# Moving a kernel's tiles so that both matmul operands start at the same offset modulo 512 bytes

## The chip, the cores and the metric

The kernel runs on one core of a Trainium2 chip. The metric is the device time of one execution in microseconds (us), as the median of several runs. The kernel's engines are TensorE (PE; its weight loads are listed as PEld), VectorE (DVE), ScalarE (ACT), GpSimd (POOL) and SyncE (SP, which only issues transfers here). They read and write the on-chip memory, of which each of the 128 partitions has its own stretch of bytes; a tile is a range of byte addresses, the same in every partition.

## The reference

One decoder layer for 256 tokens of 2048 features, all in float32:

```python
h = x @ w_in + b_in                       # 2048 -> 5120
a = a_val * sigmoid(a_gate)               # 1024 channels
a = silu(layer_norm(causal_conv31(a)))    # depthwise, 31 taps
s = sc_b * causal_conv3(sc_c * sc_h)      # depthwise, 3 taps
x = layer_norm(ALPHA * x + concat(a, s) @ w_out + b_out)
# PEER: 8 heads, 128 x 128 = 16384 experts, 16 chosen per head and token
q = x @ w_q
s = q . sub_keys; top 16 of each half; top 16 of the 256 sums -> experts, gates g
f = sum over chosen (gelu(x . u[expert]) * g) * v[expert]
x = layer_norm(ALPHA * x + f)
```

## The kernel before

The kernel computes the experts densely: it multiplies the tokens with all of u and weights the result with a matrix of gates that is zero for experts not chosen. All weights pass once through the core as a stream of 656 units of 128 x 1024 float32 (512 KB each): 80 units of w_in, 32 of w_out, 32 of w_q, 256 of u, 256 of v.

Every product is made of three matmuls. A float32 value is split into a rounded upper part (type f32r, fast on TensorE) and a rest: w = w_hi + w_lo, x = xt_hi + xt_lo. Then hi x hi, hi x lo and lo x hi are added up in the accumulation memory (psum). So each unit of the stream passes four engines: SyncE issues its load into a slot of `raw` (4 slots; from the fifth unit of v on also 3 slots of `raw_late`), ScalarE writes the upper part into one of four tiles `w_hi` (L627), VectorE writes the rest into one of four tiles `w_lo` (L843; GpSimd at L571 for the 32 units of w_q and the first 36 of u), and TensorE uses them. ScalarE may only write a w_hi when TensorE has released it (`used`), SyncE may only fill a raw slot when the rest was taken from it.

TensorE's work by stage, in program order:

- w_in, w_q and u (L1411 to L1413): a matmul loads 128 x 128 of a weight part into the array (the stationary operand, 512 bytes per partition) and streams 256 columns of xt_hi or xt_lo (the moving operand, 1024 bytes per partition). A unit has 24 such matmuls. During w_in, VectorE also computes the taps of the convolutions (L878 to L882, L973 to L997); the output projection waits for its last `mix_lo`.
- w_out (L1460 to L1462): here the loaded operand is mix_hi or mix_lo (128 tokens), and 512 columns of w_hi or w_lo are streamed (2048 bytes). 12 matmuls a unit. Then two layer-normalisation halves and transposes of the result (L1486).
- w_q: between the units the scores (L1500) load q_t and stream keys, 128 columns, two calls at a time, each as two matmuls in the profile.
- u: in the tile number 14 TensorE transposes the selections (L1542), after which every third tile has a batch of eight matmuls in 16-bit types that makes the gates (L1553).
- v, the downward stage (L1587 to L1589): coefficients c_hi, c_lo (128 tokens) are loaded, 512 columns of w are streamed. For half of the columns, only the first 128 tokens are computed this way; for the other 128 tokens GpSimd gathers the 128 chosen coefficients (L588) and rows of v (L582) by indirect transfers, and VectorE adds them up, one pick of 128 x 1024 every other unit or so (L1312). The coefficients come through a copy of `hid` in main memory, dumped by ScalarE's queue. The last four units of the stream do not go to w_hi and w_lo but to tiles of their own, `tail_hi` and `tail_lo` (`parts_of`), on the same lines.

The order within each engine is written out by hand, with semaphores between the engines. Tiles get their addresses in the order of their declaration; an ExitStack that is closed gives its space free for what is declared next, so that tiles of different stages share bytes.

Adding up the declared sizes gives these starts, in bytes modulo 512, of what TensorE reads:

| tiles | before | after |
|---|---|---|
| w_hi0 to 3, w_lo0 to 3 | 0 | 0 |
| xt_hi, xt_lo, mix_hi, mix_lo | 288 | 0 |
| c0 to c4 (hi and lo) | 288 | 0 |
| tail_hi0 to 3, tail_lo0 to 3 | 288 | 0 |
| q_t0, q_t1, oh1, oh2g | 288 | 0 |
| acc | 288 | 0 |
| keys, ident | 96 | 320 |

All steps that the matmuls of the table's first four rows take inside these tiles are multiples of 512 bytes.

Of the kernel before, what the change touches and what calls it, by code (L numbers as in the profile page):

```python
# [5 lines left out]
P = 128  # L6
T = 256
TB = T // P
D = 2048
KT = D // P  # L10
HALF = KT // 2
# [6 lines left out]
N_KEYS = 128  # L18
DCH = 512
NCH = D // DCH  # L20
GROUP = 4
GROUPS = N_KEYS // GROUP
BATCH = 8
INNER = 2
OUTER = BATCH // INNER
# [5 lines left out]
JCOLS = JOINED * DCH  # L31
NB = T // BATCH
PICKS = HEADS * TOPK
ROWS = 4
# [7 lines left out]
PARTS = 2  # L42
# [6 lines left out]
RAW = 4  # L49
SPLIT = 4  # L50
# [68 lines left out]
RAW_LATE = 3  # L119
# [47 lines left out]
def build(nc, x_t, x_nat, w_in, w_out, w_q, u_w, v_w, params, sub_keys, b_out, ln1_g, ln1_b, ln2_g, ln2_b, out):  # L167
    f32 = mybir.dt.float32
    f32r = mybir.dt.float32r
    bf16 = mybir.dt.bfloat16  # L170
    f16 = mybir.dt.float16
# [7 lines left out]
    with ctx:  # L179
        def sb(name, shape, dt, where=ctx):  # L180
            return where.enter_context(nc.sbuf_tensor(name, shape, dt))
# [1 line left out]
        def sem(name):  # L183
            return ctx.enter_context(nc.semaphore(name))

        raw = sb("raw", [P, RAW, HALF * P], f32)
        w_hi = [sb(f"w_hi{i}", [P, HALF * P], f32r) for i in range(SPLIT)]
        w_lo = [sb(f"w_lo{i}", [P, HALF * P], f32r) for i in range(SPLIT)]
        stats = sb("stats", [P, TB, NCH, 6], f32)
        mv = sb("mv", [P, TB, 2], f32)  # L190
        rstd = sb("rstd", [P, TB, 1], f32)
        neg_mean = sb("neg_mean", [P, TB, 1], f32)

        def coefs(name, where):
            return [sb(f"{name}_{part}", [P, GROUP, T], f32r, where) for part in ("hi", "lo")]


        down0 = ExitStack()
        c_sets = [coefs("c0", down0)]
        sp_coef = sb("sp_coef", [P, PICKS], f32, down0)  # L200
        row_late = sb("row_late", [P, JCOLS], f32, down0)
        down0.close()
        iota_t = sb("iota_t", [P, N_KEYS, INNER], f16)
        tab1 = sb("tab1", [P, T], f16)
        tab2 = sb("tab2", [P, T], f16)
        gate_p = sb("gate_p", [P, T], bf16)
        gate_t = sb("gate_t", [P, PARTS, T], f16)
        oh1 = sb("oh1", [P, OUTER, N_KEYS, INNER], bf16)
        gtmp = sb("gtmp", [P, N_KEYS, BATCH], f32)
        oh2g = sb("oh2g", [P, OUTER, PARTS, N_KEYS, INNER], f16)  # L210


        down1 = ExitStack()
        c_sets += [coefs("c1", down1)]
        raw_late = sb("raw_late", [P, RAW_LATE, HALF * P], f32, down1)
        rows = [sb(f"rows{i}", [P, JCOLS], f32, down1) for i in range(ROWS - 1)] + [row_late]
        down1.close()
        xt_hi = sb("xt_hi", [P, KT, T], f32r)
        xt_lo = sb("xt_lo", [P, KT, T], f32r)

        early = ExitStack()
# [48 lines left out]
        down2 = ExitStack()  # L272
        res = sb("res", [P, TB, D], f32, down2)
        ln2g = sb("ln2g", [P, D], f32, down2)
        ln2b = sb("ln2b", [P, D], f32, down2)
        c_sets += [coefs(f"c{i}", down2) for i in (2, 3, 4)]
        tail_hi = [sb(f"tail_hi{i}", [P, HALF * P], f32r, down2) for i in range(SPLIT)]
        tail_lo = [sb(f"tail_lo{i}", [P, HALF * P], f32r, down2) for i in range(SPLIT)]
        down2.close()


        def raw_of(u):
# [5 lines left out]
                return tail_hi[u % SPLIT], tail_lo[u % SPLIT]  # L288
            return w_hi[u % SPLIT], w_lo[u % SPLIT]

        hid = sb("hid", [P, N_KEYS, T], f32)

# [1393 lines left out]
```

## Time and profile before

| | |
|---|---|
| median of 3 runs | 1748.53 us (1746.63 to 1752.34) |
| span of the profiled execution | 1745.8 us (the page gives no device time of it beside the span) |
| TensorE matmul busy | 1713.3 us, 98% |
| TensorE weight load busy | 1578.1 us, 90% |
| VectorE busy | 1407.6 us, 81% |
| ScalarE busy | 854.0 us, 49% |
| GpSimd busy | 540.4 us, 31% |
| moved by transfers | 504.52 MB, mean 289 GB/s |

Busy time of TensorE is to be read with care: matmuls are pipelined, each is shown longer than the distance to the next, so that the engine counts as busy at any rate of issue. What tells the rate is the distance between two starts. A line of the profile names what is written, an arrow, and what is read; an x and a number count the instructions of a group. PEclk is the granted clock, 1.00 being 2.4 GHz.

### The profile page before, as it was taken

To read this page: it belongs to the slowest core of one execution; us is meant where nothing else is said; L and a number is where in the kernel's file an instruction comes from. 1 tells how busy PE (TensorE), PEld (TensorE's weight loads), DVE (VectorE), ACT (ScalarE), POOL (GpSimd) and SP (SyncE) were. 2 spreads that over 40 slices of the span, in tenths; PEclk is the share of its full clock that TensorE was granted. 3 is DMA by queue.
4 is the path that set the end of the run, shared out by engine and by line. 5 is a ranking of instruction groups with operands and counts; after the bars stand their busy time and mean duration, and the time that the engine had idled before them with its cause. 6 is when DMAs were issued, how large, how long until landed. Compare 5 with 4: busy or idle time off the path is not lost.

```text
span 1745.8 us, 31461 instructions
## 1 busy us (share of the span) xinstructions
PE 1713.3 (98%) x11910; PEld 1578.1 (90%) x11910; DVE 1407.6 (81%) x1998; ACT 854.0 (49%) x1084; POOL 540.4 (31%) x342
## 2 busy tenths in 40 slices
PE   8999999899999999999999999999999999999997
PEld 8999987799999999999999999998788777878776
DVE  7999997678967677777777777556899898999997
ACT  5544436344544444444444444445555555555544
POOL 0000000288881000000000000004787777777731
PEclk9999999999999999999999999999999999999999
DMA  7787787777777777777677777899899999999994
GB/s 267 267 276 267 234 260 249 273 237 235 250 249 252 238 236 244 247 235 239 237 241 239 236 244 243 282 355 332 314 400 400 399 401 389 400 399 395 369 398 133
DMA packets 173728, 504.52 MB, mean 289 GB/s; under 512 B 19408, under 2 KB 35920, under 8 KB 172624
## 3 DMA queue, kind: packets, MB, share of 16 engines
q1 hardware_dynamic: 134000, 427.08, 70.0%
q0 software_dynamic: 22528, 67.19, 10.0%
q10 hardware_dynamic: 17120, 9.35, 1.8%
q8 instruction: 29, 0.48, 0.1%
q14 instruction: 51, 0.42, 0.1%
HBM read 490.98 MB, written 79.69 MB: 327 GB/s over the span
## 4 chain that ended last, share of the span: by engine, by line
PE 78%; DMA 6%; DVE 6%; issue 5%; POOL 3%; ACT 1%; DVEq 1%; SPq 0%; POOLq 0%; ACTq 0%
PE psum L1411 18%; PE psum L1413 18%; PE psum L1412 18%; PE psum L1587 6%; PE psum L1589 6%; PE psum L1588 6%; POOL sp_coef L588 2%; DVE w_lo L843 2%; DMA raw<-in_v_w_dram 2%; PE psum L1553 2%; DMA raw_late<-in_v_w_dram 1%; PE psum L1460 1%; PE psum L1462 1%; PE psum L1461 1%; DVE psum L1312 1%
## 5 line engine op out<-in xcount | busy, mean ns | idle before, releaser
L627 ACT ACTIVATE w_hi<-raw 128x1024 fp32r<-128x1024 f32 x547 | 578.9, 1060 | 682.1 <-PE psum L1413 487.1
L1411 PE MATMUL psum<-xt_hi,w_hi 128*128 128x256 f32 x2944 | 827.2, 281 | 5.3 <-DVE xt_lo L857 3.1
L1412 PE MATMUL psum<-xt_lo,w_hi 128*128 128x256 f32 x2944 | 822.6, 279 | 0.0
L1413 PE MATMUL psum<-xt_hi,w_lo 128*128 128x256 f32 x2944 | 822.4, 279 | 0.0
L843 DVE TENSOR_TENSOR w_lo<-raw,w_hi 128x1024 fp32r<-128x1024 f32 x479 | 581.8, 1222 | 221.5 <-ACT w_hi L627 219.7
L1411 PEld LDWEIGHTS psum<-xt_hi,w_hi 128*128 128x128 f32 x2944 | 554.3, 188 | 6.6 <-issue 6.0
L1412 PEld LDWEIGHTS psum<-xt_lo,w_hi 128*128 128x128 f32 x2944 | 554.3, 188 | 0.0
L1413 PEld LDWEIGHTS psum<-xt_hi,w_lo 128*128 128x128 f32 x2944 | 554.1, 188 | 0.0
L582 POOL DMA_INDIRECT rows<-v_rows,sp_idx x96 | 130.9, 1364 | 709.7 <-issue 674.9
L1587 PE MATMUL psum<-w_hi,c_hi 128*128 128x512 f32 x752 | 299.7, 399 | 8.9 <-DVE w_lo L843 8.7
L1589 PE MATMUL psum<-w_hi,c_lo 128*128 128x512 f32 x752 | 298.2, 396 | 0.0
L1588 PE MATMUL psum<-w_lo,c_hi 128*128 128x512 f32 x752 | 297.9, 396 | 0.0
L571 POOL TENSOR_TENSOR w_lo<-raw,w_hi 128x1024 fp32r<-128x1024 f32 x68 | 164.7, 2427 | 364.3 <-ACT w_hi L627 364.2
L588 POOL DMA_INDIRECT sp_coef<-hid_spill,sp_idx x128 | 193.0, 1508 | 55.2 <-issue 45.9
L1587 PEld LDWEIGHTS psum<-w_hi,c_hi 128*128 128x128 f32 x752 | 141.7, 188 | 49.5 <-DVE w_lo L843 15.4
L1589 PEld LDWEIGHTS psum<-w_hi,c_lo 128*128 128x128 f32 x752 | 141.6, 188 | 34.3
L1588 PEld LDWEIGHTS psum<-w_lo,c_hi 128*128 128x128 f32 x752 | 141.7, 188 | 33.3
L627 ACT ACTIVATE w_hi<-raw_late 128x1024 fp32r<-128x1024 f32 x105 | 111.3, 1060 | 103.2 <-PE psum L1589 75.0
L843 DVE TENSOR_TENSOR w_lo<-raw_late,w_hi 128x1024 fp32r<-128x1024 f32 x105 | 126.6, 1221 | 8.4 <-ACT w_hi L627 8.4
L1312 DVE SCALAR_TENSOR_TENSOR psum<-rows,sp_coef,psum 128x1024 f32<-128x1024 f32 x95 | 121.8, 1282 | 3.2 <-DMA rows<-v_rows,sp_idx 2.3
L882 DVE SCALAR_TENSOR_TENSOR cacc<-apad,prm,cacc x232 | 101.3, 480 | 0.0
L1293 DVE TENSOR_TENSOR c_lo<-hid,c_hi 128x1024 fp32r<-128x1024 f32 x32 | 39.2, 1224 | 22.9 <-ACT c_hi L776 22.8
(164 smaller groups left out, 1131.8 us busy)
## 6 DMA issues: line engine op xcount, KB each, us to landing
raw<-in_u_w_dram SPq DMA_DIRECT2D x256, 512.0 KB, 4.2
raw<-in_v_w_dram SPq DMA_DIRECT2D x148, 512.0 KB, 8.7
v_rows<-in_v_w_dram SPq DMA_DIRECT2D x128, 512.0 KB, 5.2
raw_late<-in_v_w_dram SPq DMA_DIRECT2D x108, 512.0 KB, 8.9
raw<-in_w_in_dram SPq DMA_DIRECT2D x80, 512.0 KB, 4.3
raw<-in_w_out_dram SPq DMA_DIRECT2D x32, 512.0 KB, 4.5
raw<-in_w_q_dram SPq DMA_DIRECT2D x32, 512.0 KB, 4.5
hid_spill<-hid ACTq DMA_DIRECT2D x7, 1024.0 KB, 15.4
```

The source lines that it names most:

```text
L571: nc.gpsimd.tensor_tensor(w_lo[s][:, :], raw[:, s, :], w_hi[s][:, :].bitcast(f32), ALU.subtract).then_inc(lo_done[s], SPLIT)
L582: nc.gpsimd.indirect_dma_start(rows[k % ROWS][:, :], None, v_rows, bass.IndirectOffsetOnAxis(sp_idx[:, 1, k:k + 1], 0)).then_inc(rows_in[k ...
L588: nc.gpsimd.indirect_dma_start(sp_coef[:, k:k + 1], None, hid_dram, bass.IndirectOffsetOnAxis(sp_idx[:, 0, k:k + 1], 0)).then_inc(act_in[k ...
L627: nc.scalar.activation(parts_of(slot_u)[0][:, :], raw_of(slot_u), ACT.Copy).then_inc(hi_done, 1)
L843: tt(lo_w[:, :], raw_of(slot_u), hi_w[:, :].bitcast(f32), ALU.subtract).then_inc(lo_done[slot_u % SPLIT], SPLIT)
L1312: i = stt(picked[:, :], rows[k % ROWS][:, :], sp_coef[:, k:k + 1], picked[:, :], ALU.mult, ALU.add)
L1411: mm(dst, hi_w[:, sl], xt_hi[:, kk, :], start=st, stop=False)
L1412: mm(dst, hi_w[:, sl], xt_lo[:, kk, :], start=False, stop=False)
L1413: i = mm(dst, lo_w[:, sl], xt_hi[:, kk, :], start=False, stop=en)
L1587: mm(v_bank(j, b), c1, w1, start=st, stop=False)
L1588: mm(v_bank(j, b), c1, w2, start=False, stop=False)
L1589: i = mm(v_bank(j, b), c2, w1, start=False, stop=en)
```

## The change

The declarations are put in another order, and one tile is added. First come the tiles of the early stages, the routing, the accumulators and the late tiles, which all lie over the space of `hid`, then `hid` itself; behind it raw, w_hi, w_lo and the small tiles, then an unread tile `place_pad` of 56 floats (224 bytes) in each partition, then the tiles of the first coefficient sets and the gates, and xt. The list of coefficient sets has the same order as before. No instruction, wait, transfer or loop differs.

```diff
-        raw = sb("raw", [P, RAW, HALF * P], f32)
-        w_hi = [sb(f"w_hi{i}", [P, HALF * P], f32r) for i in range(SPLIT)]
-        w_lo = [sb(f"w_lo{i}", [P, HALF * P], f32r) for i in range(SPLIT)]
...
-        down0 = ExitStack()
-        c_sets = [coefs("c0", down0)]
...
-        xt_hi = sb("xt_hi", [P, KT, T], f32r)
-        xt_lo = sb("xt_lo", [P, KT, T], f32r)
         early = ExitStack()
...
-        c_sets += [coefs(f"c{i}", down2) for i in (2, 3, 4)]
+        c_late = [coefs(f"c{i}", down2) for i in (2, 3, 4)]
...
         down2.close()
+        hid = sb("hid", [P, N_KEYS, T], f32)
+
+        raw = sb("raw", [P, RAW, HALF * P], f32)
+        w_hi = [sb(f"w_hi{i}", [P, HALF * P], f32r) for i in range(SPLIT)]
+        w_lo = [sb(f"w_lo{i}", [P, HALF * P], f32r) for i in range(SPLIT)]
+        stats = sb("stats", [P, TB, NCH, 6], f32)
+        mv = sb("mv", [P, TB, 2], f32)
+        rstd = sb("rstd", [P, TB, 1], f32)
+        neg_mean = sb("neg_mean", [P, TB, 1], f32)
+        sb("place_pad", [P, 56], f32)
+
+        down0 = ExitStack()
+        c_sets = [coefs("c0", down0)]
...
+        down1 = ExitStack()
+        c_sets += [coefs("c1", down1)] + c_late
...
+        xt_hi = sb("xt_hi", [P, KT, T], f32r)
+        xt_lo = sb("xt_lo", [P, KT, T], f32r)
...
-        hid = sb("hid", [P, N_KEYS, T], f32)
```

## Rows read from the trace of the kernel before

**Rows 1.** The page's head: the profiled span.
```profile
span 1745.8 us, 31461 instructions
```

**Rows 2.** Windows by stage: length, busy time of each engine, PEclk, transfers' share, GB/s.
```profile
core 0: us, PE busy (x) PEld busy (x) DVE busy (x) ACT busy (x) POOL busy (x), PEclk, DMA share, GB/s
...
100.00:246.00 146.00, 145.13 (x1203) 142.88 (x1201) 140.24 (x251) 61.29 (x69) 0.00 (x0) 1.00 0.78 262
...
272.00:323.00 51.00, 51.00 (x219) 41.08 (x220) 34.25 (x35) 26.88 (x30) 0.00 (x0) 1.00 0.85 297
336.00:1168.00 832.00, 831.13 (x7115) 826.08 (x7116) 603.05 (x1050) 383.98 (x604) 155.29 (x64) 1.00 0.75 249
...
1248.00:1625.00 377.00, 371.42 (x1576) 295.98 (x1576) 352.60 (x315) 206.25 (x199) 289.18 (x204) 1.00 1.03 398
...
1650.00:1695.00 45.00, 44.17 (x189) 35.03 (x188) 44.02 (x41) 24.20 (x23) 17.75 (x12) 1.00 1.03 409
1695.00:1735.00 40.00, 39.80 (x172) 31.98 (x171) 30.61 (x37) 19.88 (x22) 5.11 (x4) 1.00 0.48 167
```

**Rows 3.** Waits from 12 to 246 us (first row) and 336 to 1168 (others): total, times, longest.
```profile
DVE apad L947 <- ACT sig L653: 3.6, 4, 1.5
...
ACT w_hi L627 <- PE psum L1413: 401.4, 254, 4.1
...
DVE tab L1219 <- PE psum L1542: 12.9, 1, 12.9
```

**Rows 4.** Timeline of TensorE at the end of the upward stage, first and last of 28.
```profile
1165.75 0.28 PE L1412 MATMUL psum<-xt_lo,w_hi 128*128 128x256 f32 x1
...
1168.90 0.28 PE L1412 MATMUL psum<-xt_lo,w_hi 128*128 128x256 f32 x1
```

**Rows 5.** Waits from 1248 to 1695 us.
```profile
ACT w_hi L627 <- DMA raw<-in_v_w_dram: 33.7, 32, 2.4
...
ACT w_hi L627 <- DMA raw_late<-in_v_w_dram: 24.2, 22, 1.8
```

**Rows 6.** Timeline of TensorE: 21 tail starts, then 24 ordinary, then 19 tail.
```profile
1719.65 0.39 PE L1587 MATMUL psum<-tail_hi,c_hi 128*128 128x512 f32 x1
...
1724.19 0.39 PE L1589 MATMUL psum<-tail_hi,c_lo 128*128 128x512 f32 x1
...
1724.41 0.40 PE L1587 MATMUL psum<-w_hi,c_hi 128*128 128x512 f32 x1
...
1729.78 0.40 PE L1589 MATMUL psum<-w_hi,c_lo 128*128 128x512 f32 x1
...
1731.17 0.39 PE L1589 MATMUL psum<-tail_hi,c_lo 128*128 128x512 f32 x1
...
1735.25 0.39 PE L1589 MATMUL psum<-tail_hi,c_lo 128*128 128x512 f32 x1
```

**Rows 7.** Line 1413: the one ahead of a score batch, and all from 340 to 1168 us.
```profile
L1413 PE MATMUL psum<-xt_hi,w_lo x1: 274/274/274, 360.6 to 360.6; 128*128 128x256 f32 x1
...
L1413 PE MATMUL psum<-xt_hi,w_lo x2255: 274/278/415, 340.0 to 1168.0; 128*128 128x256 f32 x188
```

**Rows 8.** The chain that ended last: start, length, what.
```profile
341.82 1.31 PE psum L1486 x12
...
1186.97 13.88 DMA hid_spill<-hid
...
1238.02 6.26 DMA rows<-v_rows,sp_idx
```

**Rows 9.** Transfers of the weights of v: issuer, count, KB, us to landing.
```profile
raw<-in_v_w_dram SPq DMA_DIRECT2D x148, 512.0 KB, 8.7
...
raw_late<-in_v_w_dram SPq DMA_DIRECT2D x108, 512.0 KB, 8.9
```

More of the change, by code:

```diff
@@ L184, in sem @@
             return ctx.enter_context(nc.semaphore(name))
-        raw = sb("raw", [P, RAW, HALF * P], f32)
-        w_hi = [sb(f"w_hi{i}", [P, HALF * P], f32r) for i in range(SPLIT)]
-        w_lo = [sb(f"w_lo{i}", [P, HALF * P], f32r) for i in range(SPLIT)]
[L189 to L192, printed above, removed]
         def coefs(name, where):
             return [sb(f"{name}_{part}", [P, GROUP, T], f32r, where) for part in ("hi", "lo")]
-        down0 = ExitStack()
-        c_sets = [coefs("c0", down0)]
[L200 to L217, printed above, removed]
-        xt_hi = sb("xt_hi", [P, KT, T], f32r)
-        xt_lo = sb("xt_lo", [P, KT, T], f32r)
         early = ExitStack()
@@ L279, in build @@
         down2.close()
+        hid = sb("hid", [P, N_KEYS, T], f32)
[9 more added lines that the diff above has]
+        c_sets = [coefs("c0", down0)]
+        sp_coef = sb("sp_coef", [P, PICKS], f32, down0)
+        row_late = sb("row_late", [P, JCOLS], f32, down0)
+        down0.close()
+        iota_t = sb("iota_t", [P, N_KEYS, INNER], f16)
+        tab1 = sb("tab1", [P, T], f16)
+        tab2 = sb("tab2", [P, T], f16)
+        gate_p = sb("gate_p", [P, T], bf16)
+        gate_t = sb("gate_t", [P, PARTS, T], f16)
+        oh1 = sb("oh1", [P, OUTER, N_KEYS, INNER], bf16)
+        gtmp = sb("gtmp", [P, N_KEYS, BATCH], f32)
+        oh2g = sb("oh2g", [P, OUTER, PARTS, N_KEYS, INNER], f16)
+        down1 = ExitStack()
+        c_sets += [coefs("c1", down1)] + c_late
+        raw_late = sb("raw_late", [P, RAW_LATE, HALF * P], f32, down1)
+        rows = [sb(f"rows{i}", [P, JCOLS], f32, down1) for i in range(ROWS - 1)] + [row_late]
+        down1.close()
+        xt_hi = sb("xt_hi", [P, KT, T], f32r)
+        xt_lo = sb("xt_lo", [P, KT, T], f32r)
         def raw_of(u):
```

## The prediction

> **What bounds the kernel now.** I read the page first, then the windows by stage, the timeline of TensorE, the waits of each stage, and last the chain and the transfers. The page gives a span of 1745.8 us [rows 1]; it shows no other time for that execution, and the three timed runs have their median at 1748.53, so 2.7 us lie around the span or between executions. I work out a saving in microseconds and take it from the median.
>
> The reader is to see in the windows that TensorE never rests for long: from 336 to 1168 us it is busy 831.13 of 832 us at the full granted clock, while VectorE has 603 and ScalarE 384 [rows 2]. In that stage ScalarE waits for TensorE 401.4 us [rows 3]: TensorE sets the time, and every nanosecond between two of its matmuls counts. Busy time hides what matters, though, because matmuls overlap. So I take the step from one start to the next. Twenty-seven steps from 1165.75 to 1168.90 make 3.15 us, 0.1167 us each, for 256 columns, which at 2.4 GHz take 0.1067 [rows 4]. Each matmul costs 10 ns more than its columns.
>
> Three places look different. From 100 to 246 us VectorE is busy 140.24 of 146 us beside TensorE [rows 2]. From 1248 to 1625 us the transfers stand at 398 GB/s with a share of 1.03, after 249 GB/s in the stage before [rows 2], and from 1650 to 1695 at 409. And ScalarE waits there for weights that are still on their way, 33.7 and 24.2 us [rows 5].
>
> **Part one, the addresses.** Nothing is added or removed that runs: same instructions, transfers, waits and queues. The extra tile is never touched. Only addresses move. Adding up the declared sizes (small tiles rounded up to 32 bytes, which the 224 of the diff bears out: 288 + 224 = 512), before the change the split weights start at 0 modulo 512 and everything they meet (xt, mix, c0 to c4) at 288; each step along them is a multiple of 512. Afterwards all are at 0.
>
> **Part two, its price.** The trace holds a pair of cases that differ in just this. The last four units of the stream go to tail_hi and tail_lo, which stand at 288 as c does: equal offsets already. Ordinary units on w_hi and w_lo, with offsets 0 and 288, run right before, same line of code, same c tiles. The ordinary ones take 23 steps from 1724.41 to 1729.78, 0.2335 each; the tail ones 18 steps from 1731.17 to 1735.25, 0.2267 each [rows 6]. That is 6.8 ns less on 512 columns. An earlier pass over the tail tiles, 20 steps from 1719.65 to 1724.19, makes 0.2270 each while VectorE is still splitting weights and normalising, so the quiet of the end isn't the cause.
>
> For 256 columns there is one hint. While a matmul streams, the weights of the next one are loaded. L1413 streams xt_hi (288), and normally w_hi (0) is loaded behind it. Ahead of a score batch it is q_t (288) instead: that matmul took 274 ns, the shortest there is, against a median of 278 [rows 7]. So the price is 4 ns there. Two readings of the tail rows are open: a price per streamed column gives 6.8 / 2 = 3.4 ns, a price per load gives 6.8. The 274 decides for the column reading; I take 3.4.
>
> The Trainium skill speaks against any gain: "TensorE: Matmul & The Clock Gate", Part 2, step 1, says that TensorE has two independent read ports, one for the streamed operand and one for the load, so that loading takes no bandwidth from the running matmul. By that the change saves 0. The 6.8 ns of the tail rows disagree, so it becomes a rival and not the forecast.
>
> **Part three, stage by stage.**
> - *0 to 246 us*, 80 units of 24 matmuls: 1920 x 3.4 = 6.5 us on TensorE. But VectorE's own work does not shrink. It waited for TensorE only through the sigmoids, 3.6 us in all [rows 3]; when these waits are gone it is the bound, and its last mix_lo gates the output projection. A matmul stream that is ahead by 18 to 29 units at these waits has gained 1.5 to 2.4 us there. I count 2 us (bounds 0 and 6.5).
> - *246 to 336 us*: until 272 a chain of VectorE and ScalarE runs beside TensorE; then 219 matmuls follow with TensorE busy 51.00 of 51 us [rows 2]: 219 x 6.8 = 1.5 us, plus some of the first hundred. I count 2 (bounds 1.5 and 384 x 6.8 = 2.6). The normalisation behind it stays.
> - *336 to 1184 us*, queries and upward projection, 288 units: 6912 matmuls x 3.4 = 23.5 us. What hid nothing before hides nothing now: VectorE at 603 of 832 would be at 603 of 809. The one fixed meeting, the selections that TensorE transposes in the fifteenth tile, had VectorE waiting 12.9 us for it [rows 3]; TensorE comes there about 5 us sooner, which uses up less than half. Transfers at a share of 0.75 have room. Bounds 0 and, with 6.8 ns, 47 us.
> - *1184 to 1248 us*, first 64 us of the downward projection: TensorE could gain 1.8 us, but the first picks wait for the dump of hid (landing 1200.85) and for the gathered rows (1238.02 to 1244.28) [rows 8], a chain that hangs on the end of the upward stage and not on TensorE's pace. I count 0.
> - *1248 to 1695 us*: 2.9% less time for the same bytes would want about 398 x 1.03 = 410 GB/s, and the rate stands flat at 398. Faster matmuls wait longer for weights. I count 0 of the stage's roughly 13 us. Would the moved tiles make transfers quicker? Those into raw (offset 0) took 8.7 us to land and those into raw_late (288) 8.9 [rows 9]; both stand in one queue, so I count 0 and allow 3.
> - *1695 to 1735 us*: transfers are down to 167 GB/s and TensorE is free: some 100 ordinary matmuls x 6.8 = 0.7 us. I count 1.
>
> Sum: 2 + 2 + 23.5 + 0 + 0 + 1 = 28.5 us. 1748.5 - 28.5 = 1720 us; the span goes to 1717.
>
> **Rivals.**
> - *The downward stage gains as well.* For: TensorE is busy 371.42 of 377 us there, so it looks like the bound too. Against: the flat rate of transfers. If all its 2256 ordinary matmuls save 6.8 ns that is 15.3 us, and with the whole 6.5 and 2.6 of the first stages (8832 x 3.4 + 384 x 6.8 + 15.3 = 48 us) the time is 1701. Chance of a good part of this (1700 to 1712): 14%.
> - *Less than 3.4 ns, or VectorE becomes the bound sooner.* Half of the price in the long stage gives about 1735. Chance 10% (1728 to 1743).
> - *The price per load, or more.* With 0 and 0 the surplus could vanish down to what a load alone takes. Twelve transposes of 128 columns took 1.31 us, 109 ns each [rows 8]; 116.7 - 109 = 7.7 ns over 6912 matmuls is 53 us, with the other stages about 60: 1688. In the Trainium skill, "TensorE: Matmul & The Clock Gate", the table of the issue gap gives 262 cycles for 256 columns, which would be the same 109; no row here shows a 256-column step so short. Against: the tail pairs, at equal offsets, still pay 13 ns on 512 columns. Chance 5%.
> - *The offset is not what matters.* The tail tiles differ in more than the offset: they lie elsewhere, among other tiles. If that made the 6.8 ns, nothing changes: 1748. Chance 8%. It is also the case in which the Trainium skill (the same page and step) is right about the ports.
> - *Slower.* Equal offsets put both reads on the same boundary at the same time, and 0 may be worse than 288, which is all that the trace shows. The place would be every matmul; were the price as large the other way, 8832 x 3.4 + 2688 x 6.8 = 48 us more, 1797. It decides when the long stage's step is above 0.117. Chance 5%.
>
> **How the numbers follow.** The forecast of 1720 (1712 to 1728) has 58%. The range 1700 to 1735 leaves out the no-effect case, the slower one, the load-bound one and a few of the 10%: about 2 in 10. A change within 0.3% (5 us) is about what a measurement here can't tell from none. Faster by more: 58 + 14 + 10 + 5 = 87%; same 8%; slower 5%.
>
> **What would show it.** The step in the upward stage goes from 0.1167 to 0.1133 (353 starts in 40 us rather than 343 by these steps); the transposes and score batches stay. Where the downward stage is undisturbed the step goes from 0.2335 to 0.2267, but its stalls on w_lo grow and its length hardly falls; the rate of transfers stays near 400. Before 246 us VectorE is busy without a gap and TensorE waits for mix_lo longer than now. I am wrong if the long stage's step does not move, if it falls below 0.112, or if the downward stage becomes 10 us shorter.

## The result, and the profile after

The changed kernel is slower: 1774.11 us (median of 4 runs, 1772.78 to 1778.28) against 1749.43 us for the kernel before beside it (4 runs), a ratio of 1.0139, 95% interval 1.0122 to 1.0156. The forecast was 1720, with a range of 1700 to 1735. The change is under 2%, but the interval lies wholly above 1, so it is a real loss of some 25 us.

The head of the page after, and two of its costliest groups (behind the bar: busy us, mean ns of one, idle us before them and what ended it):

```profile
span 1772.3 us, 31461 instructions
...
L1411 PE MATMUL psum<-xt_hi,w_hi 128*128 128x256 f32 x2944 | 838.0, 285 | 4.7 <-DVE xt_lo L857 2.7
...
L1587 PE MATMUL psum<-w_hi,c_hi 128*128 128x512 f32 x752 | 297.3, 395 | 18.7 <-DVE w_lo L843 16.8
```

The number of instructions is that of [rows 1], and the span is 26.5 us longer. The windows of the kernel after, same stretches and columns as [rows 2]:

```profile
core 0: us, PE busy (x) PEld busy (x) DVE busy (x) ACT busy (x) POOL busy (x), PEclk, DMA share, GB/s
...
100.00:246.00 146.00, 146.00 (x1199) 145.16 (x1198) 136.83 (x243) 59.63 (x67) 0.00 (x0) 1.00 0.78 255
...
272.00:323.00 51.00, 49.91 (x221) 40.99 (x220) 36.00 (x37) 28.48 (x33) 0.00 (x0) 1.00 0.78 268
336.00:1168.00 832.00, 828.86 (x6911) 823.20 (x6912) 593.65 (x1042) 374.25 (x593) 158.08 (x66) 1.00 0.74 239
...
1248.00:1625.00 377.00, 361.11 (x1554) 292.27 (x1553) 346.57 (x309) 203.54 (x196) 284.25 (x203) 0.99 1.01 384
...
1650.00:1695.00 45.00, 44.05 (x194) 35.96 (x193) 42.93 (x39) 24.04 (x24) 33.82 (x21) 1.00 1.02 390
```

From 336 to 1168 us TensorE is busy almost as before (828.86 us where it was 831.13), at the same clock, but 6911 matmuls start where 7115 did. The timeline of the kernel after, the end of the upward stage, then two starts in the downward stage, shows the steps:

```profile
1165.05 0.28 PE L1411 MATMUL psum<-xt_hi,w_hi 128*128 128x256 f32 x1
...
1168.29 0.28 PE L1411 MATMUL psum<-xt_hi,w_hi 128*128 128x256 f32 x1
...
1490.00 0.39 PE L1589 MATMUL psum<-w_hi,c_lo 128*128 128x512 f32 x1
...
1494.76 0.39 PE L1589 MATMUL psum<-w_hi,c_lo 128*128 128x512 f32 x1
```

The first pair has 27 steps in 3.24 us, 0.1200 each: 3.3 ns more than in [rows 4], where 3.4 less was forecast. The second has 21 steps in 4.76 us, 0.2267 each, just the step of the tail tiles in [rows 6]. So equal offsets cost time at 256 columns and save it at 512.

The first start of each stage in the two traces (before 9.44, 235.17, 336.87, 1183.83 and last 1735.25 us; after 9.03, 241.02, 340.92, 1209.69 and 1761.73) divides the difference of the spans (us):

| stage | before | after | difference |
|---|---|---|---|
| first matmul to output projection, 256 columns | 225.7 | 232.0 | +6.3 |
| output projection to queries, 512 columns | 101.7 | 99.9 | -1.8 |
| queries and upward projection, 256 columns | 847.0 | 868.8 | +21.8 |
| downward projection to its last matmul, 512 columns | 551.4 | 552.0 | +0.6 |

They add up to 26.9 us; the first matmul of the kernel after starts 0.4 us sooner. The third row is close to 6912 x 3.33 ns = 23.0 us; the first steps behind each batch and transpose grow by less. In the downward stage the quicker step came to nothing. The waits of the kernel after from 1248 to 1695 us show where it went (total, times, longest); the first and the last had been 12.8 and 7.4 us before:

```profile
PEld psum L1587 <- DVE w_lo L843: 23.7, 25, 4.4
...
ACT w_hi L627 <- DMA raw<-in_v_w_dram: 34.5, 33, 2.4
...
PE psum L1587 <- DVE w_lo L843: 15.0, 13, 4.0
```

TensorE waits longer for split weights. That their raw form is still on its way shows when the stretch is shifted by the 26 us by which the stage starts later: from 1274 to 1721 us ScalarE waits 41.4 and 24.7 us for it, where it was 33.7 and 24.2 [rows 5]. Shifted so, the transfers stand at 395 GB/s, and the kernel before has 396 from 1248 to 1695; the 384 and 390 above are of windows that lie earlier in the stage. VectorE's waits for gathered rows grow from 2.3 to 7.5 us in the stage.

Over the whole stage, what the steps longer than 300 ns take beyond the normal step adds up to 28.6 us, where it was 14.3 before.

A small part of this is the clock. Behind pauses of 4.4 and 3.5 us the granted clock of the kernel after falls to 0.50, the 1.2 GHz level, for 6.8 and 3.4 us, as in this window from it:

```profile
core 0: us, PE busy (x) PEld busy (x) DVE busy (x) ACT busy (x) POOL busy (x), PEclk, DMA share, GB/s
1272.00:1275.00 3.00, 3.00 (x8) 2.31 (x7) 3.00 (x4) 0.69 (x1) 2.39 (x3) 0.50 0.84 260
```

There 512 columns step by 427 ns, which costs 3.9 us of the 28.6. The kernel before has one such stretch, of 3.4 us behind a pause of 2.5 us, which costs 1.5 of its 14.3.

### The profile page after: what moved, and what is told of

Read it like the earlier page. It is cut to its first block, busy times and chain, and to the rows that moved or that the text cites. A ratio compares the mean times of both kernels' runs of the same rounds, so it can differ in the third digit from the quotient of the medians.

```text
span 1772.3 us, 31461 instructions
## 1 busy us (share of the span) xinstructions
PE 1730.0 (98%) x11910; PEld 1606.5 (91%) x11910; DVE 1408.1 (79%) x1998; ACT 854.2 (48%) x1084; POOL 543.3 (31%) x342
## 4 chain that ended last, share of the span: by engine, by line
PE 77%; DMA 8%; DVE 6%; issue 5%; POOL 3%; ACT 1%; DVEq 0%; SPq 0%; POOLq 0%; ACTq 0%
PE psum L1411 20%; PE psum L1412 20%; PE psum L1413 20%; PE psum L1587 4%; PE psum L1589 4%; PE psum L1588 4%; DVE w_lo L843 3%; DMA raw<-in_v_w_dram 2%; POOL sp_coef L588 2%; DMA raw_late<-in_v_w_dram 2%; PE psum L1553 2%; DVE psum L1312 1%; DMA row_late<-v_rows,sp_idx 1%; PE psum L1460 1%; PE psum L1461 1%
## 5 line engine op out<-in xcount | busy, mean ns | idle before, releaser
L1411 PE MATMUL psum<-xt_hi,w_hi 128*128 128x256 f32 x2944 | 838.0, 285 | 4.7 <-DVE xt_lo L857 2.7
L1412 PE MATMUL psum<-xt_lo,w_hi 128*128 128x256 f32 x2944 | 833.4, 283 | 0.0
L1413 PE MATMUL psum<-xt_hi,w_lo 128*128 128x256 f32 x2944 | 833.2, 283 | 0.0
L1411 PEld LDWEIGHTS psum<-xt_hi,w_hi 128*128 128x128 f32 x2944 | 565.3, 192 | 6.0 <-issue 5.4
L1412 PEld LDWEIGHTS psum<-xt_lo,w_hi 128*128 128x128 f32 x2944 | 565.4, 192 | 0.0
L1413 PEld LDWEIGHTS psum<-xt_hi,w_lo 128*128 128x128 f32 x2944 | 565.3, 192 | 0.0
L582 POOL DMA_INDIRECT rows<-v_rows,sp_idx x96 | 152.7, 1590 | 725.8 <-issue 692.5
L1589 PE MATMUL psum<-w_hi,c_lo 128*128 128x512 f32 x752 | 294.3, 391 | 0.0
L588 POOL DMA_INDIRECT sp_coef<-hid_spill,sp_idx x128 | 175.0, 1367 | 56.4 <-issue 47.3
L1588 PEld LDWEIGHTS psum<-w_lo,c_hi 128*128 128x128 f32 x752 | 142.1, 189 | 28.6
```

The lines of the kernel that those rows point to most:

```text
L582: nc.gpsimd.indirect_dma_start(rows[k % ROWS][:, :], None, v_rows, bass.IndirectOffsetOnAxis(sp_idx[:, 1, k:k + 1], 0)).then_inc(rows_in[k ...
L588: nc.gpsimd.indirect_dma_start(sp_coef[:, k:k + 1], None, hid_dram, bass.IndirectOffsetOnAxis(sp_idx[:, 0, k:k + 1], 0)).then_inc(act_in[k ...
L1411: mm(dst, hi_w[:, sl], xt_hi[:, kk, :], start=st, stop=False)
L1412: mm(dst, hi_w[:, sl], xt_lo[:, kk, :], start=False, stop=False)
L1413: i = mm(dst, lo_w[:, sl], xt_hi[:, kk, :], start=False, stop=en)
L1588: mm(v_bank(j, b), c1, w2, start=False, stop=False)
```

## The experiments

Theory 1 says that the step depends on the distance between the two places that TensorE reads at once, the stream's and that of the weights being loaded, and that 0 is bad for 256 columns and good for 512. Its rival, theory 2, puts the time down to the order of the tiles or to what else lies near them.

### The two reads by themselves

A kernel of its own, with no reference work: one tile of weights at offset 0 modulo 512, sixteen tiles to stream, mv_a to mv_p, at 0, 32, ... 480, nothing beside TensorE. Each is streamed with a weight load per matmul, first 64 times 256 columns, then 48 times 512.

```diff
+for mv in mvs:
+    case(mv, 256)      # st[:, k*128:(k+1)*128] loaded, mv[:, k*256:(k+1)*256] streamed
+for mv in mvs:
+    case(mv, 512)
```

> This kernel leaves the layer out and only measures: one loaded tile st at offset 0 modulo 512, sixteen streamed tiles mv_a to mv_p at offsets 0, 32, 64 ... 480, 64 matmuls of 256 columns on each and then 48 of 512 columns on each, with a load of 128 columns before every one, as in the layer; the other engines are idle. Theory 1 (the step depends on the difference of the two offsets, and differently for 256 and for 512 columns): at 256 columns mv_a (0) steps by 120 ns and mv_j (288) by 116.7 on average; at 512 columns mv_a steps by 227, and the offset that stands for 224 (mv_h) by 233.5. Theory 2 (position in the partition or the traffic of other engines makes the difference): all sixteen step alike in each width, within 1 ns. If theory 1 holds, the sweep says which difference is the cheapest for 256 columns; there may be one near 113.

The timeline of this kernel, a group for each tile (start, busy, what):

```profile
71.51 7.42 PE L66 MATMUL psum<-mv_g,st 128*128 128x256 f32 x64
78.77 7.73 PE L66 MATMUL psum<-mv_h,st 128*128 128x256 f32 x64
86.34 7.84 PE L66 MATMUL psum<-mv_i,st 128*128 128x256 f32 x64
94.01 7.71 PE L66 MATMUL psum<-mv_j,st 128*128 128x256 f32 x64
101.56 7.70 PE L66 MATMUL psum<-mv_k,st 128*128 128x256 f32 x64
...
131.88 7.42 PE L66 MATMUL psum<-mv_o,st 128*128 128x256 f32 x64
139.14 7.73 PE L66 MATMUL psum<-mv_p,st 128*128 128x256 f32 x64
...
224.68 11.35 PE L66 MATMUL psum<-mv_h,st 128*128 128x512 f32 x48
235.87 11.05 PE L66 MATMUL psum<-mv_i,st 128*128 128x512 f32 x48
246.75 11.37 PE L66 MATMUL psum<-mv_j,st 128*128 128x512 f32 x48
```

From one group's start to the next: mv_g, 192 bytes off, (78.77 - 71.51) / 64 = 113.4 ns; mv_i, 256 off, 7.67 / 64 = 119.8; mv_j, 288 off, 118.0. With 512 columns mv_i makes 10.88 / 48 = 226.7 and mv_h 233.1. Tiles that are 256 bytes apart behave alike (mv_o as mv_g), so the period is 256 bytes and not 512. Settled steps, the first few matmuls of a tile left out (of mv_a those at the lower clock too), by the distance modulo 256:

| bytes | 0 | 32 | 64 | 96 | 128 | 160 | 192 | 224 |
|---|---|---|---|---|---|---|---|---|
| 256 columns, ns | 120.0 | 117.8 | 117.8 | 120.0 | 118.7 | 117.4 | 113.3 | 118.2 |
| 512 columns, ns | 226.7 | 233.3 | 228.9 | 233.3 | 233.4 | 234.2 | 233.4 | 233.4 |

The layer's 120.0 and 226.7 are both here at distance 0, with nothing else running. That is theory 1, and it leaves VectorE, ScalarE and the transfers out of the cause. One number is a nanosecond off: mv_j has the distance of the kernel before and steps 117.8, while the layer stepped 116.7; the last sweep below finds 116.7 at this distance too.

### The order without the pad

The changed kernel without its pad: everything behind it lies 224 bytes lower, so xt, c0 and c1 are 288 from the weights again, in the new order. The mix tiles, first in the partition, stay at 0.

```diff
-        sb("place_pad", [P, 56], f32)
```

> The changed kernel without its unread tile: the new order of the tiles stays, the difference of the offsets is 288 again for xt, c0 and c1, while mix and c2 to c4 are at 0 as w is. Theory 1 (the difference of offsets): the upward stage steps by 116.7 ns as before and the time comes back to 1749 within 4 us. Theory 2 (the new place in the partition costs the time): the step stays at 120 and the time stays near 1774.

1748.92 us against 1750.94, ratio 0.9989 (0.9975 to 1.0003). The long stage steps 116.67 ns as before; the output projection steps 226.7 and takes 100.0 us, as after, since mix still stands at 0. The order by itself shows no effect.

### Only xt away from the weights

```diff
-        (stats, mv, rstd, neg_mean and place_pad behind the weights)
+        sb("x_pad", [P, 72], f32)
         xt_hi = sb("xt_hi", [P, KT, T], f32r)
         xt_lo = sb("xt_lo", [P, KT, T], f32r)
+        (stats, mv, rstd, neg_mean)
```

Weights, mix and coefficients are all at 0, xt alone at 288.

> The changed kernel with xt_hi and xt_lo alone put back to 288 by 288 unread bytes in front of them (the small tiles stand behind xt, which makes the first unread tile unnecessary); mix and all c stay at 0. Theory 1: the step of 256 columns is 116.7, that of 512 columns 227; the time is that of the kernel before less what the quicker 512-column matmuls give, 2 us in the output projection and 0 to 5 in the downward stage that its transfers bound: 1742 to 1748. If the downward stage is bound by TensorE and not by transfers: 1732. Theory 2 (place): 120 and near 1774.

1748.78 against 1750.94, ratio 0.9985 (0.9974 to 0.9997). Stage by stage it is the kernel before in the two stages on xt (225.6 and 848.7 us, where it was 225.7 and 847.0) and the kernel after elsewhere: 227.1 ns a step with 512 columns and 28.6 us of pauses in the downward stage, which is no shorter (551.9). The time lies just above the 1742 to 1748 expected. The slowdown is xt's offset alone, and the quicker steps at 512 columns are worth 2 us.

### xt at 192, the best distance of the sweep

As above with `x_pad` of 48 floats instead of 72.

> As x_at_288, with 192 unread bytes in front of xt_hi instead of 288: xt lies 192 above w modulo 256, where the sweep had its cheapest 256-column step, and mix and all c stay at the offset of w. Theory 1 (the difference modulo 256 bytes sets the step): 256 columns step by 113.3 ns, so the 288 units from the queries to the end of the upward stage take 848 - 6912 x 0.0034 = 825 us; 512 columns step by 227; the downward stage stays near 551 us, since transfers bind it; the first stage gains 1 to 3 us, since VectorE binds it. Time 1721, between 1717 and 1727. Theory 2 (in the whole layer other engines' traffic disturbs the step, so that the sweep does not carry over): 116 and more, 1745 or above.

1755.41 us against 1749.86, ratio 1.0020 (1.0004 to 1.0036), where 1721 was expected: the 113.3 ns of the sweep did not last. The 12 runs lie between 1746.28 and 1760.22; the one traced took 1759.92. The timeline of this kernel, before the first score batch and then in the upward stage:

```profile
345.04 0.28 PE L1412 MATMUL psum<-xt_lo,w_hi 128*128 128x256 f32 x1
...
347.99 0.28 PE L1411 MATMUL psum<-xt_hi,w_hi 128*128 128x256 f32 x1
...
599.94 0.28 PE L1411 MATMUL psum<-xt_hi,w_hi 128*128 128x256 f32 x1
...
602.77 0.28 PE L1411 MATMUL psum<-xt_hi,w_hi 128*128 128x256 f32 x1
```

The first pair makes 26 steps of 113.5 ns, as the sweep had it. Behind the score batch the stream falls to 24 steps in 2.83 us, 117.9, and stays there for the rest of the stage: same tiles, same addresses, another step. A score batch isn't needed for it. In the first stage, which has none, the same kernel steps 117.8 from 14 to 237 us; as many matmuls start in 40 us there as in the upward stage:

```profile
100.00:140.00 40.00, 40.00 (x342) 40.00 (x341) 39.58 (x65) 16.49 (x19) 0.00 (x0) 1.00 0.85 284
...
600.00:640.00 40.00, 40.00 (x342) 39.67 (x342) 28.22 (x41) 18.06 (x31) 0.00 (x0) 1.00 0.75 239
```

### Finer distances, and both operands moved

The sweep again with 8-byte shifts, and with a second tile of weights, `st_off`, at 64.

```diff
+# the name of the streamed tile, its offset modulo 512 (a multiple of 32) and a shift inside it, the columns
+ROWS = [("st_zero", "a", 160, 16, 256), ("st_zero", "b", 160, 24, 256), ("st_zero", "c", 192, 0, 256),
+        ("st_zero", "d", 192, 8, 256), ("st_zero", "e", 192, 16, 256), ("st_off", "f", 0, 0, 256),
+        ("st_off", "g", 64, 0, 256), ("st_zero", "h", 0, 8, 512), ("st_zero", "i", 0, 16, 512),
+        ("st_zero", "j", 224, 16, 512), ("st_off", "k", 64, 0, 512), ("st_off", "l", 256, 0, 512)]
```

> Measures only, as sweep32. Loaded tile st_zero at 0: streamed at 176 (mv_a), 184 (mv_b), 192 (mv_c), 200 (mv_d), 208 (mv_e), 256 columns; loaded tile st_off at 64: streamed at 0 (mv_f, difference 192 modulo 256) and at 64 (mv_g, difference 0), 256 columns; then 512 columns: st_zero with 8 (mv_h), 16 (mv_i) and 240 (mv_j), st_off with 64 (mv_k, difference 0) and with 256 (mv_l, difference 192). Theory 1a (the difference counts, not the address): mv_f 113.3, mv_g 120, mv_k 226.7, mv_l 233.4. Theory 1b (the streamed tile's own address counts): mv_f 120, mv_k like 64 in the first sweep (228.9), mv_l 226.7. If the unit is 64 or 32 bytes, 176 to 208 differ from one another by steps; if only whole units count, 200 equals 192. Nothing goes below 113.3 at 256 columns or 226.7 at 512.

Its timeline:

```profile
28.16 7.73 PE L74 MATMUL psum<-mv_b,st_zero 128*128 128x256 f32 x63
35.73 7.32 PE L74 MATMUL psum<-mv_c,st_zero 128*128 128x256 f32 x63
42.89 7.79 PE L74 MATMUL psum<-mv_d,st_zero 128*128 128x256 f32 x63
...
58.03 7.58 PE L74 MATMUL psum<-mv_f,st_off 128*128 128x256 f32 x63
65.44 7.71 PE L74 MATMUL psum<-mv_g,st_off 128*128 128x256 f32 x63
72.99 11.36 PE L74 MATMUL psum<-mv_h,st_zero 128*128 128x512 f32 x48
...
106.64 11.06 PE L74 MATMUL psum<-mv_k,st_off 128*128 128x512 f32 x48
117.54 11.36 PE L74 MATMUL psum<-mv_l,st_off 128*128 128x512 f32 x48
```

mv_c, 192 off, makes 7.16 / 63 = 113.7; its neighbours at 184 and 200 make 120 and 121. With both operands at 64 the step is that of distance 0 again: 119.8 at 256 columns (mv_g), 10.90 / 48 = 227.1 at 512 (mv_k). mv_l, 192 from its weights, makes 233.3, close to the 233.4 of that distance in the first sweep. So the distance counts and not the place. But mv_f, 192 from its weights as mv_c is, makes 7.41 / 63 = 117.6, where 113.3 was expected: the second step that the layer had shown, now with nothing beside it. And 8 bytes end the gain at 512 columns (mv_h, 233.3), though they lie in the same 32-byte piece as 0, so it isn't a matter of which such piece the reads begin in. At 16 bytes the step is 231.7, at 240 it is 236.7.

### Fewer gathered rows

To see what binds the downward stage, the kernels before and x_at_192 gather only the first four of v's rows and leave the other gathers out; the picks use stale rows. So the transfers carry less, GpSimd issues 124 gathers fewer, and VectorE no longer waits for rows; all else stays.

```diff
                 if k >= ROWS:
-                    pool.wait_ge(picked_done, k - ROWS + 1)
+                    return
...
-                dve.wait_ge(rows_in[k % ROWS], 16 * (k // ROWS + 1))
+                if k < ROWS:
+                    dve.wait_ge(rows_in[k], 16)
```

> The kernel before, but only the first four of the 128 gathers of v's rows are made and the later picks read those four tiles again (64 MB less to move, same work on every engine, wrong sums). Theory A (transfers bind the downward stage): with them gone TensorE runs at its own pace, 2256 x 0.2334 + 48 x 0.2267 = 537 us plus the wait for the first picks: 538 to 542 us instead of 551. Theory B (TensorE or VectorE binds it): 550 or more, as before.

> x_at_192 with the same gathers left out. Theory A (transfers bind the downward stage and swallow the quicker 512-column matmuls): 2304 x 0.2267 = 522 us plus the wait for the first picks and what VectorE with its 514 us of work adds: 525 to 533 us, about 10 less than few_rows_before. Theory B (something other than transfers swallows them): no shorter than few_rows_before.

With the old offsets: 1737.07 against 1749.86 us, ratio 0.9919 (0.9894 to 0.9944); downward stage 539.5 us with 2.3 of pauses, where it was 551.4 with 14.3. With x_at_192's: 1732.61, ratio 0.9894 (0.9869 to 0.9919); 528.9 us, where x_at_192 had 554.6. The window of the first:

```profile
core 0: us, PE busy (x) PEld busy (x) DVE busy (x) ACT busy (x) POOL busy (x), PEclk, DMA share, GB/s
1250.00:1650.00 400.00, 399.88 (x1713) 321.29 (x1712) 382.87 (x342) 224.40 (x217) 154.71 (x105) 1.00 0.80 260
```

At 260 GB/s TensorE never rests, and the quicker steps at 512 columns now shorten the stage by 10.6 us; with all gathers, at 394 to 396 GB/s over the same 447 us of the stage in the kernels before, after, x_at_288 and x_at_192, they shorten it by nothing. The gathers' load is what binds that stage. It acts through the weights: ScalarE's waits for weights still in transit, 33.7 and 24.2 us in the kernel before [rows 5], are gone. VectorE's waits for rows, 2.3 us in the stage of the kernel before, were waits for transfers as well. The lighter GpSimd doesn't speed VectorE up: its w_lo takes 1.22 us each with the gathers and without. Neither of the two kernels falls to the lower clock in the stage, which is 1.5 of the first one's 11.9 us and about 3 of the second one's 25.7.

### Does the way into a stream decide its step?

Theory 3: after a few dozen matmuls the two reads settle into a repeating pattern; some distances have more than one such pattern, and how the stream began picks one. The sweep in steps of 16 bytes, each tile twice, once from rest and once behind two matmuls of 128 columns in full float32, as the score batches are:

```diff
+pe.wait_ge(done, i + 1)
+case(i, 48)
+for b in range(2):
+    mm(psum[:, 1, b*P:(b+1)*P], raw[:, b*P:(b+1)*P], raw[:, 256:384], start=True, stop=True)
+case(i, 48).then_inc(done, 1)
```

> Measures only. Streamed tiles mv_a to mv_p lie 0, 16, 32 ... 240 bytes above the loaded tile modulo 256 (mv_m is 192), 256 columns, added up in one bank; each runs 48 matmuls from rest, then 48 behind two full-float32 products of 128 columns as in the layer's score batches. Theory 3 (the two streams of reads settle into a repeating pattern, and one difference can have more than one): mv_m steps by 113.3 ns after one start and by 117.8 after the other, as it did in sweep32 and in the layer; mv_a by 120 after both. Theory 4 (in the layer other engines' traffic spoils the good pattern): mv_m steps by 113.3 after both starts, since here nothing else runs. If some other difference steps by 113.3 after both starts, it is the one for the layer.

The timeline of this kernel, the ends of the two streams of mv_h (112) and of mv_m (192); the profile groups the settled part of a stream by itself:

```profile
120.77 3.45 PE L69 MATMUL psum<-mv_h,st_zero 128*128 128x256 f32 x29
...
126.83 3.33 PE L69 MATMUL psum<-mv_h,st_zero 128*128 128x256 f32 x28
...
180.78 3.68 PE L69 MATMUL psum<-mv_m,st_zero 128*128 128x256 f32 x31
...
186.75 3.81 PE L69 MATMUL psum<-mv_m,st_zero 128*128 128x256 f32 x31
```

Busy time less one matmul's 0.28, divided by the count less one, is the step. mv_m makes 3.40 / 30 = 113.3 from rest and 3.53 / 30 = 117.7 behind the scores: theory 3, and the layer's two steps. mv_h makes 113 ns both times. That the way in matters is thus shown; that reads settle into a pattern is the explanation that fits, and no record shows the reads. In steps of 16 bytes, settled (ns, from rest / behind scores):

| 0 | 16 | 32 | 48 | 64 | 80 | 96 | 112 |
|---|---|---|---|---|---|---|---|
| 120 / 120 | 118.7 / 116.7 | 116.7 / 116.8 | 118.4 / 118.3 | 117.8 / 117.8 | 118.2 / 118.4 | 119.9 / 119.9 | 113.3 / 113.3 |

| 128 | 144 | 160 | 176 | 192 | 208 | 224 | 240 |
|---|---|---|---|---|---|---|---|
| 118.5 / 120.0 | 116.6 / 116.7 | 117.4 / 118.6 | 119.2 | 113.3 / 117.8 | 119.0 | 118.4 / 118.3 | 117.2 / 117.2 |

"From rest" and "behind scores" name the two ways in of this sweep and are no rule. In x_at_192 the first 22 matmuls behind the kernel's start stepped 117.7, and in few_rows_192, the same up to there, 113.9. And 288 bytes has two steps in the layer as well: in no_pad and x_at_288, of the streams between two score batches every other one steps 117.8, the rest 116.6.

### xt at 112

```diff
-        xt_hi = sb("xt_hi", [P, KT, T], f32r)
-        xt_lo = sb("xt_lo", [P, KT, T], f32r)
+        sb("x_pad", [P, 24], f32)
+        xt = sb("xt", [P, 4 + 2 * KT * T], f32r)
+        xt_hi, xt_lo = (xt[:, 4 + i*KT*T:4 + (i+1)*KT*T].rearrange("p (k t) -> p k t", t=T)
+                        for i in range(2))
```

96 bytes of pad and 16 inside the tile; all else is as in x_at_192.

> As x_at_192, but xt lies 112 bytes above w modulo 256 (96 unread bytes, and both halves in one tile behind 16 more). Theory 3 (two streams of reads that settle into a repeating pattern; at 112 both starts of the sweep ended in the 113.3 ns one, after about 20 matmuls): undisturbed stretches of the layer step by 113.3 (354 starts in 40 us against 345), the 144 matmuls between two gate batches by about 114, the 48 between score batches by about 115.5. From the queries to the end of the upward stage 848 - 6144 x 0.0027 - 768 x 0.0012 = 830 us. The first stage gains 1 to 3 us, VectorE being busy; the downward stage stays near 551. Time 1730 us, between 1724 and 1736. Theory 4 (traffic spoils it): 116.7 or more and 1748.

1725.39 us (1722.81 to 1729.66) against 1750.13, ratio 0.9867 (0.9843 to 0.9890): faster than both kernels. Its timeline in the upward stage and its window:

```profile
640.03 0.28 PE L1412 MATMUL psum<-xt,w_hi 128*128 128x256 f32 x1
...
643.77 0.28 PE L1412 MATMUL psum<-xt,w_hi 128*128 128x256 f32 x1
```

```profile
600.00:640.00 40.00, 40.00 (x354) 39.54 (x353) 28.86 (x40) 19.31 (x34) 0.00 (x0) 1.00 0.77 248
```

33 steps in 3.74 us, 113.3 each. Behind each score batch the first 30 steps make 115.1 on average, then it is 113.3 again. 354 matmuls start in this window, against 337 of the kernel after:

```profile
600.00:640.00 40.00, 40.00 (x337) 39.68 (x336) 27.96 (x38) 18.14 (x32) 0.00 (x0) 1.00 0.75 232
```

The queries and the upward projection take 826.7 us, 20.3 less than before; the first stage 221.5, 4.3 less. The output projection takes 101.7 us and not 99.9, since TensorE waits longer for the last mix_lo in it.

## Why the prediction was wrong

**The step that failed** is the price for 256 columns: "The 274 decides for the column reading; I take 3.4." It had the wrong sign. 8832 matmuls of 256 columns cost 3.3 ns more each, 29 us; the two stages on xt grew by 6.3 + 21.8 = 28.1.

Two things made the step weak. The tail rows [rows 6] are a fair pair, but of 512 columns: their 6.8 ns held wherever 512 columns met offset 0 (226.7 in the sweep, 226.9 to 227.3 in the layer). Halving it assumes that the price runs with the columns. It doesn't: distance 0 is the best of all at 512 columns and among the worst at 256. And the one hint at 256 columns [rows 7] was the duration of one matmul. Steps in this stream aren't equal: in the kernel before they go round through 113, 116, 118 and 120 ns, with 116.7 as their mean, so one short matmul may be any of them. In the kernel after, where q_t, too, is at xt's offset, all matmuls of line 1413 from 356 to 367 us, around the same spot:

```profile
L1413 PE MATMUL psum<-xt_hi,w_lo x29: 279/283/283, 355.9 to 366.8; 128*128 128x256 f32 x29
```

Their minimum, 279, is above the 274 and even the median of 278 that [rows 7] show, and the two ahead of score batches (358.38 and 364.57 us) took 283 each. Equal offsets are not what made the 274.

**The rival with 5%** named the mechanism, equal offsets being worse than 288, and the point where it decides (a step above 0.117). Its 1797 was too high because it took 6.8 ns for the 512 columns too, and those gained.

**The rival "the offset is not what matters"** is refuted by the sweep and by no_pad. The port rule of the Trainium skill ("TensorE: Matmul & The Clock Gate", Part 2, step 1), by which a load takes no bandwidth from the running matmul, does not fit these runs: with nothing else running, steps of 256 columns lie between 113.3 and 121 ns by the distance of the two operands. What in the two reads meets was not seen, and no run streams without loads. The rival of a price per load needed steps near 109 ns; no distance went below 113.3.

**Stages.**
- *Queries and upward stage*: that TensorE binds it was right; x_at_288 and x_at_112 turn the price of a step straight into time. Forecast -23.5, measured +21.8.
- *First stage*: -2 forecast of a possible -6.5, since VectorE was to be the bound; measured +6.3. A longer step makes TensorE the bound there and counts in full (1920 x 3.3 ns = 6.3 us). For a shorter one the cover by VectorE was about right: x_at_112, with 3.3 ns less a step, gained 4.3 us, and TensorE's wait for the last mix_lo then grew from 1.1 to 3.0 us, which leaves 2.4.
- *Output projection*: -2 forecast, -1.8 measured.
- *Downward stage*: 0 forecast, +0.6 measured. That transfers bind it, that the step falls to 0.2267 and that the stalls on w_lo grow was right, and the few-rows pair shows it. What it left out is the lower clock behind the longer pauses, 2.4 us more of it than before. The 14% rival, that this stage gains as well, falls with it.

**What stays open.** Why the same distance has several settled patterns, and which reads meet in them, was not seen: no record shows a single read. The patterns are read from the steps alone. Nor was it tried whether 112 holds with weights elsewhere than at 0.

## What to carry to other kernels

A single matmul's duration is no rate: take the mean step over some dozens of starts, and only for the shape and the operands whose price is wanted. Where the bound is a TensorE stream with a load per matmul, a stand-alone sweep over the distance of its two operands modulo 256 bytes, in steps of 16, entered as the kernel enters it, costs one run and here pointed to 25 us. It shows which distances to try and not which will hold: 192 was its best and failed in the layer. What a quicker stream gives is then decided by each stage's own bound.

## What was unexpected of the hardware

- In float32r with a load for each matmul, the step of 256 columns runs from 113.3 to 121 ns and that of 512 from 226.7 to 236.7, by the distance of the two operands' addresses modulo 256 bytes; 8 bytes can be the whole difference (120, 113.3 and 121 at 184, 192 and 200).
- The order of distances is another for each width: 0 is best for 512 columns and costs 120.0 at 256; 192 costs 113.3 and 233.4.
- A stream can be in one of two steady paces on the same addresses (113.3 or 117.8 at 192) and keep it for hundreds of microseconds; two short matmuls in another format are enough to change it, and the layer entered the slower one without them as well.
- In the downward stage each of the ten stretches at a granted clock of 0.50 (3.4 or 6.8 us long, 427 ns a step with 512 columns) began in a pause or within 1.4 us behind a pause of TensorE of 2.4 to 4.5 us, and cost 1.3 to 2.8 us beyond it. Not every pause of that length had one: that of 3.2 us at 1461 us in x_at_192 had none.
